# One program per layer for norm, input product, four mixers and output product, with attention in pairs of heads

## What is computed

```
n = rms_norm(h, g_mix) * (1 + scale) + shift
z = n @ w_in                        # 1376 columns: fourier 256, q latent 192, kv latent 128, rope key 32, gate 512, pool 256
y = concat(
    fourier(z_f),                   # fft over tokens and over 64 head channels, real part, then a 64x64 product per head
    attention(q, k, v),             # 4 heads of 64 + 32 (rope), q = rms_norm(z_q) @ w_uq; k, v = rms_norm(z_kv) @ w_ukv
    gating(z_g),                    # gelu, rms_norm of v per head, a 128x128 product over tokens, + b, times u
    pooling(z_p))                   # window means of 2, 4, 8, 16 tokens minus z, a 64x64 product per group
h = h + gate * (y @ w_out)
```

## Time and profile before

| | us |
|---|---|
| runs (3): median, lowest, highest | 5076.97, 5075.85, 5081.25 |
| the profiled execution: its own time | 5076.53 |
| its span, first to last instruction | 5074.7 |
| TensorE MATMUL records: busy | 4525.5 (89% of the span), 39776 records |
| VectorE, ScalarE, GpSimd busy | 1666.6, 1237.3, 61.1 |
| mean granted TensorE clock | 0.943 of 2.4 GHz |

### The profile page before, as it was taken

One profiled execution on the slowest core, in us unless ns is written; L12 is line 12 of the kernel. 1 busy time (PEld: TensorE's weight loads), 2 busy tenths in 40 slices (PEclk: granted clock), 3 DMA queues, 4 the chain that ended last, 5 costly groups with the idle time before them and its releaser, 6 DMA issues. The chain is left out here.

```text
span 5074.7 us, 86250 instructions
## 1 busy us (share of the span) xinstructions
PE 4525.5 (89%) x39776; PEld 3449.9 (68%) x39776; DVE 1666.6 (33%) x2146; ACT 1237.3 (24%) x1798; POOL 61.1 (1%) x65
## 2 busy tenths in 40 slices
PE   7999999988799978999895788999899997767998
PEld 4666666665477756888753457888788885434886
DVE  4555555551233323222303313222322222132333
ACT  2333333320344423212101203112221211122222
POOL 0000000000000000000002000000000000200000
PEclk9999999998899988999997688999899998888999
DMA  3000000022444331121111001121111110101222
GB/s 146 8 16 20 20 20 20 20 86 107 163 165 167 143 132 67 57 73 53 35 50 43 0 33 67 55 75 52 61 59 63 67 55 34 59 1 66 84 104 71
DMA packets 45329, 331.76 MB, mean 65 GB/s; under 512 B 4401, under 2 KB 8882, under 8 KB 21298
## 3 DMA queue, kind: packets, MB, share of 16 engines
q1 hardware_dynamic: 44978, 326.37, 17.5%
HBM read 324.26 MB, written 2.10 MB: 64 GB/s over the span
## 5 line engine op out<-in xcount | busy, mean ns | idle before, releaser
L714 PE MATMUL banks<-x_hi,w_hi 128*128 128x512 f32 (+1 forms) x2464 | 860.4, 349 | 30.0 <-DVE x_lo L815 30.0
L715 PE MATMUL banks<-x_lo,w_hi 128*128 128x512 f32 (+1 forms) x2464 | 856.1, 347 | 0.0
L716 PE MATMUL banks<-x_hi,w_lo 128*128 128x512 f32 (+1 forms) x2464 | 854.4, 347 | 0.0
L714 PEld LDWEIGHTS banks<-x_hi,w_hi 128*128 128x128 f32 x2464 | 471.6, 191 | 105.0 <-DVE x_lo L815 28.6
L716 PEld LDWEIGHTS banks<-x_hi,w_lo 128*128 128x128 f32 x2464 | 471.9, 192 | 57.3
L715 PEld LDWEIGHTS banks<-x_lo,w_hi 128*128 128x128 f32 x2464 | 472.7, 192 | 54.2
L715 PE MATMUL banks<-g_lo,w_hi 128*128 128x512 f32 (+1 forms) x1232 | 423.9, 344 | 0.0
L714 PE MATMUL banks<-g_hi,w_hi 128*128 128x512 f32 (+1 forms) x1232 | 423.6, 344 | 0.0
L716 PE MATMUL banks<-g_hi,w_lo 128*128 128x512 f32 (+1 forms) x1232 | 423.3, 344 | 0.0
L725 ACT CAST w_hi<-landing 128x2048 fp32r<-128x2048 f32 (+1 forms) x152 | 255.7, 1682 | 494.4 <-PE banks L716 494.4
L993 PE MATMUL banks<-x_normed_first,weight_ring_first 128*128 128x256 f32 (+1 forms) x1024 | 365.1, 498 | 5.3 <-ACT small L1363 2.6
(11 more groups left out here) (393 smaller groups left out, 5682.0 us busy)
## 6 DMA issues: line engine op xcount, KB each, us to landing
arena_first<-in_ada_w SPq DMA_DIRECT2D x44, 2048.0 KB, 7.6
landing<-in_w SPq DMA_DIRECT2D x88, 1024.0 KB, 4.8
landing<-in_w SPq DMA_DIRECT2D x64, 704.0 KB, 4.1
weight_ring_first<-in_rw_pair SPq DMA_DIRECT2D x8, 2048.0 KB, 8.1
weight_ring_first<-in_da_head SPq DMA_DIRECT2D x8, 2048.0 KB, 12.1
weight_ring_mix<-in_w_in SPq DMA_DIRECT2D x12, 1024.0 KB, 4.9
weight_ring_first<-in_ada_w SPq DMA_DIRECT2D x4, 2048.0 KB, 8.8
weight_ring_mix<-in_w_out SPq DMA_DIRECT2D x8, 1024.0 KB, 4.9
```

The lines of the kernel that those rows point to most:

```text
L714: nc.tensor.matmul(o, wh, xh[:, k, c0:c0 + cn], start=k == 0, stop=False)
L715: nc.tensor.matmul(o, wh, xl[:, k, c0:c0 + cn], start=False, stop=False)
L716: ins = nc.tensor.matmul(o, wl, xh[:, k, c0:c0 + cn], start=False, stop=k == kt - 1)
```

## The change

`mixers`, `local_mixers` and `latent_attention` go, and `mixing` comes, one block with one program per engine; the calls of `norm` and of both `linear` go with them.

- **Norm**: as in the feed-forward halves. The squares lie in the normed tiles' own buffer, TensorE sums each block of 128 tokens into one column, root and reciprocal are taken of 128x6, and TensorE spreads them by products with the identity. VectorE multiplies x, gain and root in one instruction per segment, ScalarE shifts.
- **Input product**: 11 tiles of 128 columns, since the upper part of q and the rope key share one (tile 3). In the last layer only tiles 3 and 4 (kv) are made for the context. Tiles 2, 3 and 4 go first and together, each row tile of the norm as it is ready. The others are "pieces".
- **Pieces**: 44 in layer 0 and 24 in layer 1, products of one bank each: the tiles of z by segment (`w`), the gate's sums (`vsum`), the head transform (`zc`), the token transform (`f`), `fw`, the gate's transposes (`vt`) and products (`sg`), and `pool`. They use banks 6 and 7 in turn; a piece waits until the one two before it has been evacuated. `f`, `fw` and `sg` are evacuated by VectorE, the others by ScalarE, in the program order of these engines. A few pieces stand between the steps of the preparation (`prep`), the others are dealt out by weight to two slots in each pair.
- **Pairs**: two heads by 128 queries, 12 in layer 0 and 8 in layer 1. TensorE's order in a pair: the scores of both heads, slot a, the transposes of both, slot b, the values of both. The two heads' value products alternate between the two halves of the array's columns. ScalarE evacuates the first head's transposes, VectorE the second's, into the banks' successors; the next pair's scores wait for both.
- **Loads**: groups of w_in, the tables, mix_w and w_out are issued by SP in one stream, each behind the last reader of its place; the tables have a place of their own in a smaller ring, since the arena shrinks from 25216 to 23040 columns.
- **GpSimd** also copies the rope key to the four heads and squares the gate's v.
- **Output product**: 8 tiles one after the other over four double banks, with its first two groups loaded before.

The signals' names change places; no other line of the untouched parts does. The diff, cut to its core:

```diff
+    def mix_pieces(self, segs):
+        each = [(x, n) for x, (_, n) in enumerate(segs)]
+        nb = (segs[-1][0] + segs[-1][1]) // P
+        out = [("w", tile, x, KT * n / 597) for tile in (0, 1, 8, 9, 6, 7, 10, 11) for x, n in each]
+        out += [("vsum", j, x, n / 597) for j in range(2) for x, n in each]
+        out += [("zc", t, 0, 0.9) for t in range(nb)]
+        out += [("f", j, x, 2 * (n // P) * n / 597) for j in range(2) for x, n in each]
+        out += [("fw", j, x, n / 597) for j in range(2) for x, n in each]
+        out += [("vt", t, 0, 0.6) for t in range(nb // 2)] + [("sg", t, 0, 0.9) for t in range(nb // 2)]
+        out += [("pool", j, x, n / 597) for j in range(2) for x, n in each]
+        return out
+    def mix_slots(self, pieces, first, pairs):
+        shares = [w for _, qt in pairs for w in ((1.0, 0.7) if qt < LAT // P else (0.5, 0.3))]
+        total, slots, n, done, due = sum(p[3] for p in pieces[first:]), [], first, 0.0, 0.0
+        for s, w in enumerate(shares):
+            due += w / sum(shares) * total
+            slot = []
+            while n < len(pieces) and (done + pieces[n][3] / 2 <= due or s == len(shares) - 1):
+                slot.append(n)
+                done += pieces[n][3]
+                n += 1
+            slots.append(slot)
+        return slots[0::2], slots[1::2]
...
+    def mixing(self, layer, last, gain, shift, scale, gate):
...
+        w_order = (2, 3, 4, 0, 1, 8, 9, 6, 7, 10, 11)
+        first_segs = (segs, BOTH, BOTH)
...
+        pairs = [(hp, qt) for hp in range(2) for qt in range(nb)]
+        keys = lambda qt: (0, NB) if qt < LAT // P else (LAT // P, NB)
+        prep = ([0, 1], [2], [3], [4], [5, 6]) if S == 2 else ([0], [1], [], [2], [3])
+        in_a, in_b = self.mix_slots(pieces, sum(map(len, prep)), pairs)
+        by_dve = ("f", "fw", "sg")
...
+                load_in(0)
+                load_in(1)
+                table(0)
+                sp.dma_start(mixw, self.dram["mix_w"][layer]).then_inc(mixw_ready.h, 16)
+                load_in(2)
+                for n in (1, 2):
+                    table(n)
+                load_in(3)
+                for n in (3, 4):
+                    table(n)
+                load_in(4)
+                load_in(5)
...
+                def first_tiles():
+                    for k in range(KT):
+                        pe.wait_ge(hn_ready.h, hn_ready.at(0, k + 1))
+                        for i in range(3):
+                            w = weights(i)
+                            for x, (c0, n) in enumerate(first_segs[i]):
+                                ins = mm(bank(2 * i + x, n), w[:, k], HN[:, k, c0:c0 + n], start=k == 0, stop=k == KT - 1)
+                            if k == KT - 1:
+                                ins.then_inc(w_done.h, 1)
...
+                def piece(n):
+                    kind, j, x, _ = pieces[n]
+                    b, (c0, size) = 6 + n % 2, segs[x]
+                    if n >= 2:
+                        s, count = piece_out(n - 2)
+                        pe.wait_ge(s.h, s.at(0, count))
+                    if kind == "w":
+                        i = w_order.index(j)
+                        w = weights(i)
+                        for k in range(KT):
+                            ins = mm(bank(b, size), w[:, k], HN[:, k, c0:c0 + size], start=k == 0, stop=k == KT - 1)
...
+                def scores(p):
+                    hp, qt = pairs[p]
+                    if p:
+                        pe.wait_ge(at_a.h, at_a.at(0, p))
+                        pe.wait_ge(at_v.h, at_v.at(0, p))
+                    for c in range(2):
+                        for c0, n in (BOTH if qt < LAT // P else BOTH[1:]):
+                            ins = mm(bank(2 * c, T)[:, c0:c0 + n], QH[0:96, 2 * hp + c, qs(qt)], KH[0:96, 2 * hp + c, c0:c0 + n], start=True, stop=True)
+                        ins.then_inc(s_done.h, 1)
+                def transposes(p):
+                    for c in range(2):
+                        pe.wait_ge(pn.h, pn.at(0, 2 * p + c + 1))
+                        for t in range(*keys(pairs[p][1])):
+                            ins = nc.tensor.transpose(bank(2 * c, T)[:, t * P:t * P + P], Pr[:, c, t * P:t * P + P], ident)
+                        ins.then_inc(pt_done.h, 1)
+                def values(p):
+                    hp, qt = pairs[p]
+                    pe.wait_ge(at_a.h, at_a.at(0, p + 1))
+                    pe.wait_ge(at_v.h, at_v.at(0, p + 1))
+                    if p:
+                        pe.wait_ge(o_out.h, o_out.at(0, p))
+                    t0, t1 = keys(qt)
+                    for t in range(t0, t1):
+                        for c in range(2):
+                            ins = mm(bank(4, P)[half(c)], Vt[:, t, half(2 * hp + c)], AT[:, c, t * P:t * P + P], start=t == t0, stop=t == t1 - 1)
+                            if c == 0 and t == t1 - 1:
+                                even = ins
+                    return even, ins
...
+                first_tiles()
+                pieces_of(prep[0])
...
+                pieces_of(prep[1])
...
+                pieces_of(prep[2])
...
+                for i in range(4):
+                    if i == 2:
+                        pe.wait_ge(kr_ready.h, kr_ready.at(0, 1))
+                    head(i)
+                pieces_of(prep[3])
...
+                for p in range(len(pairs)):
+                    scores(p)
+                    pieces_of(in_a[p])
+                    transposes(p)
+                    pieces_of(in_b[p])
+                    for ins in values(p):
+                        ins.then_inc(pv_done.h, 1)
...
+                    if n == gelus_at:
+                        act.wait_ge(piece_a.h, piece_a.at(0, taken(n)))
+                        for tile in (8, 9, 6, 7):
+                            nc.scalar.activation(Z[:, tile, 0:C], Z[:, tile, 0:C], ACT.Gelu_apprx_tanh).then_inc(gelu.h, 1)
...
+                for p in range(len(pairs)):
+                    ks = slice(keys(pairs[p][1])[0] * P, T)
+                    for c in range(2):
+                        act.wait_ge(mx.h, mx.at(0, 2 * p + c + 1))
+                        nc.scalar.activation(Pr[:, c, ks], bank(2 * c, T)[:, ks], ACT.Exp, bias=stat[:, p, 2 + c:3 + c], scale=scale_qk,
+                                             accum_out=stat[:, p, 4 + c:5 + c]).then_inc(p_ready.h, 1)
+                    take_all(in_a[p])
+                    act.wait_ge(pt_done.h, pt_done.at(0, 2 * p + 1))
+                    nc.scalar.copy(AT[:, 0, ks], bank(0, T)[:, ks]).then_inc(at_a.h, 1)
+                    take_all(in_b[p])
...
+                take_all(prep[4])
+                for p in range(len(pairs)):
+                    hp, qt = pairs[p]
+                    ks = slice(keys(qt)[0] * P, T)
+                    st = stat[:, p]
+                    for c in range(2):
+                        dve.wait_ge(s_done.h, s_done.at(0, 2 * p + c + 1))
+                        L(nc.vector.reduce_max(st[:, c:c + 1], bank(2 * c, T)[:, ks], axis=AX))
+                        L.mark(nc.vector.tensor_scalar_mul(st[:, 2 + c:3 + c], st[:, c:c + 1], -scale_qk), mx)
+                    for c in range(2):
+                        dve.wait_ge(p_ready.h, p_ready.at(0, 2 * p + c + 1))
+                        L(nc.vector.reciprocal(st[:, 6 + c:7 + c], st[:, 4 + c:5 + c]))
+                        L.mark(nc.vector.tensor_scalar_mul(Pr[:, c, ks], Pr[:, c, ks], st[:, 6 + c:7 + c]), pn)
+                    if p - vsum_pair in (1, 2):
+                        gate_norm(p - vsum_pair - 1, 0)
+                    take_all(in_a[p])
+                    dve.wait_ge(pt_done.h, pt_done.at(0, 2 * p + 2))
+                    nc.vector.tensor_copy(AT[:, 1, ks], bank(2, T)[:, ks]).then_inc(at_v.h, 1)
+                    if p - vsum_pair in (1, 2) and S == 2:
+                        gate_norm(p - vsum_pair - 1, 1)
+                    take_all(in_b[p])
+                    dve.wait_ge(pv_done.h, pv_done.at(0, 2 * p + 2))
+                    nc.vector.tensor_copy(Z[:, 2 + hp, qs(qt)], bank(4, P)).then_inc(o_out.h, 1)
...
-                K.mixer_buffers(scope, f"mix{layer}")
-                K.norm(BOTH, gain("g_mix"), m(3), m(4), K.x3(K.HN))
-                out = K.mixers(layer, last)
+                K.mix_buffers(scope, f"mix{layer}")
+                K.mixing(layer, last, gain("g_mix"), m(3), m(4), m(5))
                 if upto == f"mix{layer}":
-                    return K.final_debug(K.arena)
-                K.linear("w_out", KT // 2, KT, out, segs, "residual", gate=m(5), index=layer)
...
+    w_in = cat([w_in[..., 256:448], w_in[..., 576:608], z(32), w_in[..., 448:576], w_in[..., 0:256], w_in[..., 864:1120],
+                w_in[..., 608:864], w_in[..., 1120:1376], z(P)], -1)
+    out["w_in"] = w_in.reshape(DEPTH, KT, P, 6, 2, P).transpose(0, 3, 2, 4, 1, 5)...
```

761 lines of the change are left out of this document (387 added, 374 removed).

## The result

The changed kernel takes 4726.14 us, median of 4 runs (4724.91 to 4733.35), beside 5078.9 us of the kernel before (4 runs, 5075.85 to 5081.25): a ratio of 0.930, 95% interval 0.929 to 0.932. The profiled execution took 4726.04 us with a span of 4724.2.

The account below looks back on a forecast made before the run. TensorE was taken to wait for VectorE and ScalarE or run at reduced clock in half of the mixings' 986.3 us; less 342.5 and 268.8 leaves 375 saved, 23 given back: 5076.5 - 352 = 4724.5, forecast 4725 us, range 4690 to 4795.

Parts of the forecast that it names:

- 23 had been given back: Both layers: allowance subtracted from the 375 us saving, 0.5 us a pair for skipped hops and 13 us for clock.
- Front, first tiles, output: Stretches around preparation and pairs: front 18 us a layer, first three tiles 33 and 29.5, output with tail 84.1 and 56.3.
- its own products: Preparation: TensorE's products other than pieces (sums, key, heads, values, rotations), 27 us in layer 0, 22.8 in layer 1.
- allowance of 0.5 us a pair for skipped hops: All 20 pairs: time added for hops the summed steps leave out, bounds 0 and 1 us a pair.
- Rival B: Values in the pairs: array halves do not overlap, 0.118 us a record, 24 us in all, 4749 us; chance 0.07.
- the formula: Pair length from slot work a, b: latent 5.3 + max(2.75, a) + max(1.25, b), context 1.95 + max(2.1, a) + max(0.7, b).
- 6.5 more: Layer 0's pairs 6, 7, 10 and 11: small pieces wait for the one two before and for ScalarE, 6.5 us.
- clock as 5% of the pairs' time: Pairs of both layers: 13 us allowed for reduced clock, bounds 0 and 67 us.
- the four such instructions in each layer's pairs fall behind slots longer than they are: Pairs beside GpSimd: VectorE's two-operand instructions, slowed from 0.75 to 1.57 us, are hidden by longer slots.
- C: Rival for the pairs: pieces between steps hide nothing, pairs cost 300 instead of 257 us, 4768 in all; chance 0.11.
- D: Rival for the pairs: clock stays at 0.69 and 0.81, 67 us more instead of 13, 4779 in all; chance 0.12.
- the estimate of 6 us: Pairs: by the skill's drain rule, about 0.16 us for two mode changes in each of 20 pairs, giving 4731 us.

Follow-up runs that it names:

- norm_apart: The changed kernel with the old norm back as its own block before the first three tiles: ratio 0.9373 to the kernel before the change.
- the three together: The changed kernel with w_in pieces of 256 columns, gelus last in their pair and three banks for pieces: ratio 0.9260 to the kernel before the change.

## Why the prediction was right

The forecast was 4725 us, and its mechanism is what the traces show. That the size agrees to 1 us is partly luck, since errors cancel: the pairs took 15.9 us over their steps where 23 had been given back, the preparations 6.2 over where nothing had, and 3.8 went to the unchanged stretch before.

- **Front, first tiles, output.** 18, 33, 29.5 and the output products came within 0.5 us each. Undoing the norm alone gave 15.6 us a layer where the step had 15.5.
- **Preparation.** "Preparation without a TensorE wait over 2 us" held; the pieces cover VectorE's chain. The term that was mis-sized is "its own products", priced by columns at 0.86 for 512. A q-head product takes 1.03 and one of 256 columns 0.60, 0.17 more each; 16 of them in layer 0 make 2.7 of the 4.1 us over, 8 in layer 1 make 1.4 of 2.1, and the q sums, which alternate in the same way, 0.7 and 0.3 (rows below).
- **Pairs with a long slot.** 13.58 for 13.45, a bare pair 9.4 for 9.3. The allowance of 0.5 us a pair for skipped hops was too large: it is 0.1 to 0.4.
- **Values.** 0.055 us a record as taken. Rival B was priced at 24 us; the same products with one head behind the other cost 14, since a part of them overlaps even so.
- **Small pieces.** Layer 0's pairs 6 to 11 were to be 66.0 by the formula and 6.5 more; they took 76.6. A third bank takes 4.1 off, 1.2 of it with the clock of pair 11. The 6.5 that stay were not taken apart; the rows have pieces waiting for what they read (copies, roots), which the prediction did not cost.
- **Layer 1's pairs.** 114.7 forecast, 125.4 measured: pair 1 3.9 us over the formula where 2.6 stood for gelus and table, pair 2 5.2 over where nothing stood, pair 5 1.6 over for VectorE beside GpSimd, pair 7 5.3 over for 3.3, at a clock of 0.90. The step that failed in part is the one that gave clock as 5% of the pairs' time in both layers: it was 0.99 in layer 0, and in layer 1 mostly one fall behind one stall. That "the four such instructions in each layer's pairs fall behind slots longer than they are" was nearly right: GpSimd costs 1.8 us in both layers, and in pair 5 it is mostly the normalising (3.35 us for two heads, 1.24 without the averages), which the prediction had left out, and less the gate's scaling (1.08 for 0.75).
- **Rivals.** What C and D priced, waits that nothing covers and a low clock, are both real in this program, 47 and 32 us, as soon as the pieces leave their slots; in the change as made they show in pairs 1, 2 and 7 of layer 1 and pair 11 of layer 0. D was argued against by the 90% of work in layer 0's pairs, and that is what the clock rows show: 0.99 there, 0.92 in layer 1 with 86% busy.
- **The array's modes.** A change between 128 and 64 output rows does cost something: the record before it is followed after 0.203 us instead of 0.109 (from the values to the next scores in every pair, and in the kernel before from the last transpose at 4600.62 to the first value at 4600.82 of the earlier trace rows, where the prediction saw no pause), or after 0.522 instead of 0.429 (from a piece to the values, at 4199.53). That is 0.09 us, and at most 3.7 us for the 40 changes in the pairs, less where the values wait for a copy anyway. The sum did not miss it, because its 1.45 us for the values count the last record with its whole tail, 0.27; measured are 1.46 from the first value to the next scores (2693.07 to 2694.53). So the Trainium skill, "TensorEngine Tiling (Array Packing)", Key Properties, is right that a change of mode is not free, and the estimate of 6 us by it was too high by a third or more.
- **Table loads.** Again 1.28 us and the activation 1.29 us after the load's start (4159.27 to 4160.56); the load starts where the copy before it ends (4159.25), so there is no drain on either side, against the Trainium skill, "ScalarE: Activation LUTs", What ACT_TABLE_LOAD costs. The row that the prediction took this from the earlier trace rows had ScalarE idle for 16.41 us before the load and could not have shown a drain ahead of it.
- **What was not undone.** Of the 354 us the runs isolate the norm (31 us), the columns (21), the place of the pieces (79) and the order of the values (14), and the rows the pairing of heads (73, which holds the order of the values). That the rest comes from loads beside the work and from mixers and preparation that no longer go stage by stage, as the prediction had it, is read from the stretches and was not undone by itself.

## What to carry to other kernels

Put the independent products between the steps of a latency-bound chain, not before or after it: the same work gave 79 us by its place, 47 from covered waits and 32 from a clock that stays up. Then look at what every evacuating engine has queued ahead of the copy that the chain waits for (here four gelus and a table load), and cut the filling so fine that no slot is empty; with a third bank and the split of the gate's scaling these gave another 22 us, of which pieces of 256 columns alone gave 17. Columns that are dropped save time only where TensorE was the bound: here 21 of 27.5 us. Before crediting a few microseconds to an edit, look whether the granted clock of the same pair differs, and whether the edit has moved something else as well; both happened here.

## What was not expected of the hardware

Products of layer 1's preparation on TensorE, start and length; 128*96 is rows of contraction by output rows:

```profile
4101.14 1.10 PE L2371 MATMUL banks<-arena_mix,weight_ring_mix 128*96 128x512 f32 x2
4102.17 1.10 PE L2372 MATMUL banks<-arena_mix,weight_ring_mix 64*96 64x512 f32 x2
4103.19 1.10 PE L2371 MATMUL banks<-arena_mix,weight_ring_mix 128*96 128x512 f32 x2
...
4116.42 5.37 PE L2375 MATMUL banks<-arena_mix,weight_ring_mix 128*64 128x512 f32 x16
4121.73 3.51 PE L2445 MATMUL banks<-weight_ring_mix,arena_mix 128*128 128x256 f32 x12
```

Where the rows of contraction alternate between 128 and 64, each product starts 1.03 us after the one before, for 0.86 by its columns, its two records 0.51 and 0.52 apart. The kernel before is the control: its q heads (L2331) have the same columns and output rows but 128 rows of contraction throughout, and at a clock of 1.00 their records start 0.43 apart, 0.86 a product. The q sums alternate too, with 128 output rows on both sides, and have records 0.52 to 0.53 apart. So it is the switch of rows between 128 and 64, about 0.17 us each time; one between 96 and 128 (scores to pieces) costs nothing. A switch of output rows alone is the 0.09 us of the section on the prediction: the k heads, with one on either side, take (4121.73 - 4116.42)/4 = 1.33 for 768 columns, near the 1.29 of the others. The Trainium skill, "TensorEngine Tiling (Array Packing)", Key Properties, has a drain at a mode change and does not tell these apart.

Beside GpSimd, VectorE's one-operand normalising with a scalar per partition took 1.92 and 1.43 us for 0.62, not only the two-operand instructions of the earlier trace rows; reciprocals (3.34) and maxima (0.96) from PSUM kept their times.

How the clock answers to a single stall was not foreseen, nor is it settled. The 3.55 us of pair 1 in layer 1 were followed by some 16 us at half rate; stalls of 2.54 and 2.51 us in pairs 4 and 5 of the same trace were followed by work at full rate; and those of 2.13 and 2.64 us in the three together by values at half rate (2.83), as was the 2.52 us stall of pair 5 in norm_apart, whose program is the same there as the changed kernel's. What else distinguishes them was not tried. The same pair of the same program thus differs by up to 5 us between executions of kernels that differ elsewhere, which is more than several of the effects looked for here.
